# Attention stage of a hybrid decoder layer: the score products of a long selected unit are issued from the eighth block of the unit two before it, by columns first

## The reference

```
s_c   = q . kcmp - slope * distance;   p_c = softmax(s_c);   o_cmp = p_c @ vcmp
imp   = sum over the 4 heads of p_c @ overlap        # 32 blocks of 64 keys
sel   = the 8 blocks of highest imp (first, own and previous block forced)
o_sel = softmax(q . ks - slope * distance, over the keys of sel, causal) @ vs
o_win = softmax(q . kw - slope * distance, over the last 512 keys) @ vw
y     = gate0 * o_cmp + gate1 * o_sel + gate2 * o_win
```

## Time and profile before

| | |
|---|---|
| median of 3 runs | 4451.53 us (4450.72 to 4459.46) |
| the profiled execution | 4457.25 us, its span 4455.5 us |
| attention with the tiles `aq_...` | about 1674 to 2720 us of the span |
| mean granted TensorE clock | 0.935 of full speed |
| PE, DVE, ACT, POOL busy over the span | 3931.1, 2445.6, 1986.3, 555.2 us |

### The profile page before, as it was taken

The page is one execution under the profiler, slowest core; times in us unless marked ns, Lnnn a source line. Parts: engine busy times, 40 slices in busy tenths (PEclk is TensorE's granted clock), DMA queues, the critical chain, the costliest instruction groups (busy, mean ns, idle before and its releaser), DMA issues. The chain is left out here.

```text
span 4455.5 us, 69868 instructions
## 1 busy us (share of the span) xinstructions
PE 3931.1 (88%) x26848; PEld 3203.8 (72%) x26849; DVE 2445.6 (55%) x4139; ACT 1986.3 (45%) x3142; POOL 555.2 (12%) x842
## 2 busy tenths in 40 slices
PE   7899999999988848888888876999689999999698
PEld 5687877777766627676667765899578888887587
DVE  2455555554555416677676644444476555567465
ACT  2433333433333216566565643222166455566465
POOL 0111121111212001111111111100111000001110
PEclk9999999999998959999999976999789999999899
DMA  4443443433423150000000003433278666689542
GB/s 131 131 112 101 132 120 94 127 103 89 110 73 90 51 127 13 10 15 15 15 20 17 20 10 109 146 128 119 99 290 322 226 230 236 236 324 354 223 143 92
DMA packets 512952, 557.22 MB, mean 125 GB/s; under 512 B 106285, under 2 KB 374573, under 8 KB 511629
## 3 DMA queue, kind: packets, MB, share of 16 engines
q1 hardware_dynamic: 471476, 457.94, 32.1%
q0 software_dynamic: 16416, 59.78, 3.6%
q10 hardware_dynamic: 24784, 35.71, 2.5%
HBM read 439.78 MB, written 113.57 MB: 124 GB/s over the span
## 5 line engine op out<-in xcount | busy, mean ns | idle before, releaser
L523 PE MATMUL fr_fb<-fr_hT_h,fr_w_h 128*128 128x512 f32 (+1 forms) x1312 | 532.7, 406 | 7.7 <-DVE fr_hT_r L978 6.0
L523 PE MATMUL fr_fb<-fr_hT_h,fr_w_r 128*128 128x512 f32 (+1 forms) x1312 | 531.9, 405 | 0.0
L523 PE MATMUL fr_fb<-fr_hT_r,fr_w_h 128*128 128x512 f32 (+1 forms) x1312 | 531.7, 405 | 0.0
L958 DVE TENSOR_TENSOR fr_w_r<-fr_w_raw,fr_w_h 128x1024 fp32r<-128x1024 f32 (+1 forms) x164 | 198.1, 1209 | 491.4 <-ACT fr_w_h L774 490.3
L1885 DVE TENSOR_TENSOR aq_p_lo<-aq_t_bank,aq_p_hi 128x512 fp32r<-128x512 f32 x412 | 282.0, 690 | 260.1 <-ACT aq_p_hi L1775 257.2
L1775 ACT CAST aq_p_hi<-aq_t_bank 128x512 fp32r<-128x512 f32 x412 | 240.1, 585 | 356.3 <-PE aq_t_bank L1689 354.4
L798 ACT COPY fr_zs<-fr_fb 128x512 f32<-128x512 f32 (+1 forms) x148 | 87.1, 589 | 507.0 <-PE fr_fb L523 506.6
L523 PEld LDWEIGHTS fr_fb<-fr_hT_h,fr_w_h 128*128 128x128 f32 (+1 forms) x1312 | 248.5, 189 | 72.1 <-issue 10.4
L523 PEld LDWEIGHTS fr_fb<-fr_hT_h,fr_w_r 128*128 128x128 f32 (+1 forms) x1312 | 248.5, 189 | 63.6 <-issue 11.3
L134 PE MATMUL ex_gu<-wx_gate_w,ex_xT 128*128 128x512 f32 x1176 | 289.3, 402 | 4.7 <-DVE ex_xT L2641 4.7
L523 PEld LDWEIGHTS fr_fb<-fr_hT_r,fr_w_h 128*128 128x128 f32 (+1 forms) x1312 | 248.6, 190 | 62.1 <-issue 9.6
(11 more groups left out here) (474 smaller groups left out, 8778.2 us busy)
## 6 DMA issues: line engine op xcount, KB each, us to landing
wx_raw<-in_w_exp_gate_up SPq DMA_DIRECT2D x64, 2048.0 KB, 10.4
fr_w_raw<-in_w_in SPq DMA_DIRECT2D x160, 512.0 KB, 3.8
wx_raw<-in_w_exp_down SPq DMA_DIRECT2D x32, 2048.0 KB, 10.3
s_z<-fr_zs SPq DMA_DIRECT2D x160, 256.0 KB
s_rows<-ex_y ACTq DMA_DIRECT2D x50, 512.0 KB, 4.4
mx_mg<-s_z SPq DMA_DIRECT2D x32, 512.0 KB, 7.3
fr_zc<-s_z SPq DMA_DIRECT2D x15, 903.0 KB, 6.9
fr_x_t<-in_x SPq DMA_DIRECT2D x16, 512.0 KB, 5.2
```

The lines of the kernel that those rows point to most:

```text
L523: ins = pe.matmul(bank[0:cols_, :], (w_h, w_h, w_r)[p][:, k, c, 0:cols_].bitcast(F32R), (hT_h, hT_r, hT_h)[p][:, c, :].bitcast(F32R), star ...
L958: dve.tensor_tensor(w_r[:, m % 2, :, 0:cols_].bitcast(F32R), w_raw[:, m % 2, :, 0:cols_], w_h[:, m % 2, :, 0:cols_], ALU.subtract).then_in ...
```

## The change

For selected units from the fifth unit on with t of at least 8 (`reused`; these are units 5, 7, ... 33, 15 of them), the runs begin with the eighth block of the selected unit two before, as soon as the first eight blocks (the first 1024 columns) of the shared buffer have been transposed. The runs go by columns first: the four heads' first 1024 columns, then the second columns. `mask` waits for just the blocks whose columns it overwrites. A local unit before such a unit has its four runs in the first seven steps of the selected unit before it. The pair's work in `misc` moves with it: `out` goes to seven steps ahead of the first run, which is the first step of a selected unit, `turn` two steps earlier, into the fourth step of a local unit, where `back` also stands. The order by columns also holds for unit 3, whose runs stay in the local unit before it. Units from 34 on keep their steps.

```diff
-    Y_RING, FRONTS_APART = 3, 7
+    Y_RING, FRONTS_APART, TABLE_STEPS = 3, 7, 7
...
-        self.runs_at, self.run_end = {}, []
+        self.runs_at, self.run_end, self.begin = {}, [], []
+        for u in range(len(self.units)):
+            self.begin.append(self.first_run(u))
...
-            runs = [(h, at, min(RUN, width - at)) for h in range(Q_PER_KV) for at in range(0, width, RUN)]
+            runs = [(h, at, min(RUN, width - at)) for at in range(0, width, RUN) for h in range(Q_PER_KV)]
+            begin, end = self.begin[u], f[u] - 2
+            if self.reused(u + 1):
+                end = min(end, self.begin[u + 1])
             for i, (h, at, wide) in enumerate(runs):
-                step = f[u - 1] + i * max(f[u] - f[u - 1] - 2, 1) // len(runs) if u else -1
+                step = begin + i * max(end - begin, 1) // len(runs)
+                if self.reused(u):
+                    step = max(step, f[u - 2] + self.blocks_over(u, at + wide) - 1)
...
-            later = min(f[self.at[t, g, SEL] - 1] - 4, later - self.FRONTS_APART)
+            u = self.at[t, g, SEL]
+            later = min(self.begin[u] - (self.TABLE_STEPS if self.reused(u) else 4), later - self.FRONTS_APART)
...
-            pool += [(out - 4, 0, n, "normalise", t, g), (f[self.at[t, g, SEL] - 1], 1, n, "bias", t, g)]
+            pool += [(out - 4, 0, n, "normalise", t, g), (self.begin[self.at[t, g, SEL]] - 2, 1, n, "bias", t, g)]
...
+    def reused(self, u):
+        return 5 <= u < len(self.units) and self.units[u][2] == self.units[u - 2][2] == SEL and self.units[u][0] >= RUN // P
+
+    def first_run(self, u):
+        f = self.first
+        if not u:
+            return -1
+        return f[u - 2] + RUN // P - 1 if self.reused(u) else f[u - 1]
+
+    def blocks_over(self, u, columns):
+        return min(columns // P, self.first[u - 1] - self.first[u - 2])
...
-                        dve.wait_ge(turned, F.first[u - 1])
+                        dve.wait_ge(turned, F.first[u - 2] + F.blocks_over(u, at + wide) if F.reused(u) else F.first[u - 1])
...
-                        dve.wait_ge(s_read, i)
+                        dve.wait_ge(s_read, i - R + 1)
```

## The result

The changed kernel takes 4475.33 us (median of 5 runs, 4472.57 to 4486.62), the kernel before 4453.83 (5 runs, 4450.72 to 4462.55). The ratio is 1.0047, with a 95% interval of 1.0031 to 1.0064: slower by some 21 us, inside the range (4428 to 4488) and 19 us above the point forecast.

What follows compares the result with a forecast made beforehand. Local units were taken as bound by DVE, then ACT, selected units by PE. 47 - 66 + 21 + 2.5 = +4.5 us on the profiled 4457.25 gives 4461.8; that execution lies 5.7 above its median, so 4456 us, range 4428 to 4488.

Steps and rivals of the forecast that it cites:

- the case called likeliest: Whole kernel: even, savings in local units given back in selected units and to the clock; 4443 to 4460 us, chance 0.38.
- local units, full clock, and clock: 15 local units: shrink by 66 us at full clock as ACT becomes the bound, less 21 us for low clock.
- selected units 3 to 31: 15 selected units: moved runs add 73.5 us of PE work, partly filling its idle time; 374 against 326.5 us, +47.
- head (forecast: unit 3's late exponentials): Unit 3: its exponentials start behind the fifth mask, not the second; at most 4 us later, taken as +2.5.
- hand schedule: Local units laid out by hand at full clock: 13.6 us for unit 4, 12.0 for 10 blocks, 194 for all 15.
- clock term: Local units: PE's gaps bring one low-clock stretch each, costing 1.4 us, +21 us over 15 units.
- The 20 us more that I had attached to it: Local units: by the skill's rule, a second low-clock stretch in each would raise the sum by about 20 us.
- PE was short of work for 326 - 276 = 50 us: Selected units before the change: PE idle 3.4 us in each, of which 2.0 would remain after it.
- rival B: Slower, 4476 to 4497 us: two low-clock stretches in local units, or 3.4 us of waits per selected unit; chance 0.34.
- late next: End of local units: `back` is held about 2.3 us because `turn` before it in the one bank waits for ACT.
- rival C: Faster, 4430 to 4441 us: `oT` comes earlier in selected units, or low clock falls beside waits for ACT; chance 0.28.
- Rival D: Masks of moved runs wait for `tg` or transposed blocks, at most 1 us each; inside the even case's 0.38.

Runs made afterwards that it cites:

- experiment 3: Changed kernel plus unread matmuls in local units 4 to 32, 8 ahead of the first value product and 5 ahead of `back`: 4456.14 us, ratio 1.0000.
- experiment 1: Changed kernel with unit 3's runs head by head again, with the old wait in its masks: 4474.0 us, ratio 1.0029.
- experiment 8: Changed kernel with `turn` a step earlier, `pct` ahead of exponentials, unit 3 head by head: 4434.35 us; with filler (8 unread matmuls per local unit): 4436.3 us.
- experiment 6: Changed kernel with `turn` one step earlier and `pct` ahead of the exponentials of its step on ACT: 4444.26 us, ratio 0.9963.
- the repaired pair's work without the moved runs: Kernel before with `misc` work moved as in the changed kernel, but `turn` a step earlier and `pct` ahead of exponentials; runs unmoved: 4465.6 us, ratio 1.0019.

## Why the prediction was right in sign of its terms and low in their sum

The forecast was +4.5 us against the profiled time, 4461.8; the medians say +21.5. The time lies in the range, but the case called likeliest, a difference below 0.2%, did not come: the excess is 20 us in the profile, made of the terms below. By its own terms:

| term | forecast, us | measured in the profile, us |
|---|---|---|
| local units, full clock, and clock | -66 + 21 = -45 | -45.3 |
| selected units 3 to 31 | +47 | +56.2 |
| head (forecast: unit 3's late exponentials) | +2.5 | +9.3 (units 1 and 2) |
| units from 33 on | 0 | +4.3 |
| sum over the attention | +4.5 | +24.5 |

*Local units: right, the clock term partly by luck.* The hand schedule gave 194 us at full clock; experiment 3 has 195.9. The clock term was 21; it is 18.7 in the local units and 22.5 over units 4 to 33. How it came about was less simple: with 2 x (1 - clock) x length for each window, the 15 local units spent 80 us at the low level, against 20 before, not the 51 of one stretch like the earlier trace rows in each. The low level was longer than I thought and cheaper for each us: 18.7 us for 80, where half, 40, would be lost if PE had been at work throughout. That part of it fell where PE waited anyway is the likely reason. The rule of the Trainium skill, "TensorE: Matmul & The Clock Gate", section "A second HAM failure mode: psum-queue depth-cycling", says that short idle gaps between groups of matmuls, with PSUM banks used in turn, make the clock swing. The trace agrees in kind: 14 of the 15 local units, with stops of PE between their groups of matmuls, have a low clock (0.64 to 0.88), and the 80 us are more than one stretch of 3.42 us in each. The 20 us more that I had attached to it did not come.

*Selected units: the term that was mis-sized.* The step that failed is "PE was short of work for 326 - 276 = 50 us". I had added up unit costs to 276; the row beside it already said 293.92, so the idle time was 32.6. Of the 17.4 us between the two, some 14 are low clock, by an estimate: the windows of the earlier trace rows hold 28 us at the low level by 2 x (1 - clock) x length, at half speed, while the unit costs come from rows at a clock of 1.00. The added work looks right by the rows: PE's busy time rose by 65.9 us, against 73.5 - 6 = 67.5. The idle time that is left, 382.62 - 359.84 = 22.8, is 1.5 us for each unit and even less than the 2.0 I had assumed. So only 9.8 us of idle time were filled where the sum has 20. At a clock of 1.00 throughout, in experiment 3, the selected units take 379.06 us with PE busy for 355.17: there the unit costs (344) are 11 us short and the idle time (23.9 in place of 30) gives 6 back, against a forecast of 374. The other 3.6 us of the changed kernel are nearly all unit 29, 24.65 us at a clock of 0.83 in place of 21.80. The "decides when the selected units' sum passes 380 us" of rival B came true, but not by its mechanism (3.4 us of waits each, where 1.5 were measured); nor did its 20 us for a longer low clock come.

*The head: missed.* I priced `back` behind `pct` only in the units whose runs move, at 2.3 us. The pair's work of unit 5 begins in unit 2. PE's order of that very unit stood before me, with the two as neighbours, and I put no price on it: there `pct` stood behind two exponentials in a row, and PE stopped for 6.48 us in a unit that I had left at no change. The +2.5 for unit 3's late exponentials was right in size (2.4 in experiment 1). The other 5.0 of unit 2's 7.4 us belong to `turn` and `back`: with `turn` apart, `pct` first and unit 3 head by head, unit 2 takes 17.96 us (experiment 8 with filler), against 17.36 before. Unit 1 grew by 1.9 us, since PE's other work for the pair moved into it (71 to 82 records).

*What the forecast did not ask.* `back` behind `pct` was in my account as "late next", a fixed price inside the 194. It was not fixed: taken away (experiment 6), the local units fall to 181.1 us even with the clock at 0.95, and to 178.2 with experiment 8's kernel. Splitting the change into its two parts would have given some -31 and +52 in place of one small sum, and a change whose sum is the small difference of two such terms can be turned round by one step of the plan. The times of rival C, 4430 to 4441, are where the repaired kernel lies.

*The bounds.* Their sum is off by 5 us: selected units 348 for 374 and clock 0 for 21 give -47, not -42, and 395 and 41 give +41, not +46. Rival C's 4414 has the same slip.

*The signs in the profile.* The waits for DVE in the attention are 25.7, not under 10; in units 4 to 33 they are 7.4. `back` on `pct` is 39.6 (some 30 forecast). The stops that I had put at the transposes on `p_lo` are at the value product on `oT`: 36.4 us in the local and 20.6 in the selected units, where the hand schedule had seen only the second. Local sum 214.6 in 194 to 222; selected sum 382.6, just over the 365 to 380, with PE busy for 94% and DVE at 19.6; clock 0.92, lower as forecast. Rival D did not show: no wait of a mask for `tg` stands in the list of the attention.

*What stays open.* The last 4.3 us from unit 33 on, and the 4.9 outside the attention, are work that did not change, at a slightly lower clock in this one execution; the medians hold only part of it. Why the repaired pair's work without the moved runs is still 0.2% slower than before (its selected units are 10.6 us longer) was not taken apart.

## What to carry to other kernels

When a change drags other work along with what it is meant to move, price and run the two apart: here the runs gained some 31 us and the pair's work lost 52. Where one bank is handed from user to user, list who frees it and what stands ahead of that on the freeing engine's queue, in every unit that the new place touches, also the first. And take an engine's idle time in a stretch from its busy row, never from a sum of unit costs, and see at which clock row and costs were taken.

## What was new about the hardware

Filling stops of PE with matmuls that nobody reads raised the granted clock of units 4 to 33 from 0.92 to 1.00 and took 22.5 us off them, though PE did some 200 matmuls more. By the ratios (1.0047 and 1.0000) it is 21. The same trick gained nothing at a clock of 0.95 (551.60 and 552.16 us), where low clock then fell into later units, and lost 0.35% in the kernel before, where stops shorter than the filler's 1.9 us were filled too.
